# SSD rows in a fourth buffer and asked for earlier, attention steps in another order

## The reference, cut to what matters

```python
a_cs = jnp.cumsum(jnp.moveaxis(a, 2, -1), axis=-1)
seg = a_cs[..., :, None] - a_cs[..., None, :]
Lm = jnp.exp(jnp.where(lower, seg, -jnp.inf)).astype(xs.dtype)
cb = jnp.einsum('bclgn,bcsgn->bcgls', Cc, Bc)
y_diag = jnp.einsum('bcgls,bcgrls,bcsgrp->bclgrp', cb, Lm, x)
```

## Time and profile before

| what | us |
|---|---|
| median of 3 runs (3908.04 to 3921.22) | 3914.33 |
| the profiled execution, whole | 3913.21 |
| its span in the trace | 3911.4 |
| PE busy (12600 matmuls) | 3627.2 (93%) |
| DVE busy | 1151.3 (29%) |
| ACT busy | 767.0 (20%) |
| POOL busy | 428.8 (11%) |
| mean granted TensorE clock, of full speed | 0.978 |

### The profile page before, as it was taken

One profiled execution on the slowest core, in us unless ns is written; L12 is line 12 of the kernel. 1 busy time (PEld: TensorE's weight loads), 2 busy tenths in 40 slices (PEclk: granted clock), 3 DMA queues, 4 the chain that ended last, 5 costly groups with the idle time before them and its releaser, 6 DMA issues.

```text
span 3911.4 us, 33012 instructions
## 1 busy us (share of the span) xinstructions
PE 3627.2 (93%) x12600; PEld 1750.7 (45%) x12600; DVE 1151.3 (29%) x2612; ACT 767.0 (20%) x1772; POOL 428.8 (11%) x393
## 2 busy tenths in 40 slices
PE   8999999999999798788888788999999989999999
PEld 3555555444444433233332344555444545454444
DVE  3355656333201303110111034433221144432211
ACT  2135454223201200000000022222110122221100
POOL 0003324011000000000000002101220021012200
PEclk9899999999999899999999999999999999999999
DMA  8413223112224599999999961012222211122220
GB/s 282 154 61 97 87 72 103 49 56 87 65 65 178 212 409 409 409 409 409 409 409 409 409 236 54 27 44 81 85 76 74 76 54 38 38 92 77 74 81 27
DMA packets 302209, 634.08 MB, mean 162 GB/s; under 512 B 32554, under 2 KB 145818, under 8 KB 301798
## 3 DMA queue, kind: packets, MB, share of 16 engines
q1 hardware_dynamic: 241278, 592.28, 40.7%
q10 hardware_dynamic: 60776, 39.70, 3.7%
HBM read 625.50 MB, written 10.24 MB: 163 GB/s over the span
## 4 chain that ended last, share of the span: by engine, by line
PE 55%; DMA 17%; DVE 3%; SPq 1%; issue 1%; POOL 0%; ACT 0%; DVEq 0%
PE psum L308 27%; DMA arena<-in_w_exp_up_dram 7%; DMA arena<-in_w_exp_gate_dram 6%; PE psum L1638 6%; PE psum L2441 5%; PE psum L2898 4%; PE psum L2934 4%; DMA arena<-in_w_exp_down_dram 4%; PE psum L1462 2%; PE psum L2919 1%; PE psum L1490 1%; PE psum L2367 1%; PE psum L1471 1%; SPq L277 1%; PE psum L2833 1%
## 5 line engine op out<-in xcount | busy, mean ns | idle before, releaser
L308 PE MATMUL psum<-arena 128*128 128x512 f32 (+1 forms) x3200 | 1302.9, 565 | 2.6 <-POOL arena L2040 2.4
L308 PEld LDWEIGHTS psum<-arena 128*128 128x128 f32 x3200 | 609.8, 193 | 675.3 <-issue 653.0
L2441 PE MATMUL psum<-arena 128*64 128x512 f32 x3072 | 692.9, 597 | 141.7 <-DMA arena<-in_w_exp_up_dram 77.1
L2441 PEld LDWEIGHTS psum<-arena 128*64 128x64 f32 x3072 | 232.4, 136 | 583.3 <-issue 567.5
L1638 PE MATMUL psum<-arena 128*128 128x512 f32 x768 | 351.0, 612 | 0.0
L810 PE MATMUL psum<-arena 128*128 128x512 f32 (+1 forms) x768 | 255.9, 491 | 1.1 <-DVE arena L550 1.1
L1638 PEld LDWEIGHTS psum<-arena 128*128 128x128 f32 x768 | 147.0, 195 | 193.4 <-issue 192.5
L1570 DVE CUSTOM_DVE_ANT_0 arena<-psum,arena 128x512 f32<-128x512 f32 (+3 forms) x224 | 113.9, 546 | 391.2 <-PE psum L1462 391.0
L2977 POOL TENSOR_SCALAR arena<-arena 128x512 f32<-128x512 f32 x88 | 138.6, 1576 | 697.7 <-ACT arena L2956 697.7
L810 PEld LDWEIGHTS psum<-arena 128*128 128x128 f32 x768 | 144.4, 191 | 107.9 <-issue 96.1
L2983 DVE SCALAR_TENSOR_TENSOR arena<-arena 128x512 f32<-128x512 f32 x88 | 66.2, 752 | 426.5 <-POOL arena L2977 426.5
(11 more groups left out here) (276 smaller groups left out, 2909.4 us busy)
## 6 DMA issues: line engine op xcount, KB each, us to landing
arena<-in_w_exp_gate_dram SPq DMA_DIRECT2D x128, 1024.0 KB, 18.6
arena<-in_w_exp_up_dram SPq DMA_DIRECT2D x128, 1024.0 KB, 18.5
arena<-in_w_exp_down_dram SPq DMA_DIRECT2D x128, 1024.0 KB, 18.5
arena<-in_w_in_dram SPq DMA_DIRECT2D x64, 1024.0 KB, 5.2
arena<-in_w_up_dram SPq DMA_DIRECT2D x88, 512.0 KB, 4.9
arena<-in_w_ada_dram SPq DMA_DIRECT2D x24, 1024.0 KB, 9.1
arena<-in_w_down_dram SPq DMA_DIRECT2D x20, 1024.0 KB, 5.1
arena<-acs_scratch ACTq DMA_DIRECT2D x64, 256.0 KB, 4.6
```

What stands on the lines that cost most here:

```text
L308: mm = pe.matmul(shaped(b, l, r), l, r, start=kt == 0, stop=kt == nkt - 1)
L2441: mm = pe.matmul(banks[n][64 * j:64 * j + 64, :], lhs[:, kt, 64 * j:64 * j + 64], w, start=kt == 0, stop=kt == 2 * nkb - 1)
```

## The change

The halves with `k % 4 == 3` (n = 3 and 7 of each group) get their rows in two of the `XD` buffers, those which the last two state matmuls of the group have read; `ER` and `RB` serve the other three. The rows of halves n+2 and n+3 are both asked for after the exponents of n and n+1, and none before them. Both transfers of a half are now waited for together, before its first exponent. New waits keep the shared buffers in order: ACT waits for the state matmul 9 of the group before it asks for the rows of n = 3 or 7, DVE and POOL wait for the last use of these buffers before they weigh the sources 2 and 3 of the next group. In the attention DVE takes `weights` of the unit before ahead of `scores`, and POOL does `second` one step earlier, ahead of the filler of the following step.

```diff
--- before.py
+++ after.py
@@ -1121,6 +1121,8 @@
                 wait_xs(e, g)
             if xd_before(u):
                 e.wait_ge(*at(*xd_before(u)))
+            if g and m in (2, 3):
+                e.wait_ge(*(at("yd", g - 1, 3, 1) if m == 3 else at("sel", g - 1, 7)))
             if g == 0 and m < 2:
                 e.wait_ge(*at("ws"))
             first_xd(e, u)
@@ -1165,7 +1167,7 @@
             pe.wait_ge(*at("M", g, n))
             for h in range(4):
                 hh = 4 * hq + h
-                mm = pe.matmul(y[:, hh * 64:hh * 64 + 64], r3(ER[n_of(g, n) % 3], 128)[:, h, :], xs2[g % 2][:, c, hh * 64:hh * 64 + 64], start=True, stop=True)
+                mm = pe.matmul(y[:, hh * 64:hh * 64 + 64], r3(rows_of(n_of(g, n), 0), 128)[:, h, :], xs2[g % 2][:, c, hh * 64:hh * 64 + 64], start=True, stop=True)
             mm.then_inc(*up(S("pe_y"), ("yd", g, c, hq)))
             if hq == 0:
                 return
@@ -1191,15 +1193,18 @@
                 act.wait_ge(*at("acD"))
                 act.wait_ge(*at("gam", 5, 1))
                 act.wait_ge(*at("full", ("row", 5, 1)))
-            if k > 2:
-                act.wait_ge(*at("yd", (k - 3) // 8, (k - 3) % 8 // 2, (k - 3) % 2))
-                act.wait_ge(*at("sel", (k - 3) // 8, (k - 3) % 8))
+            if n % 4 == 3:
+                act.wait_ge(*at("full", ("st", g, 9)))
+            if k > 3:
+                act.wait_ge(*at("yd", (k - 4) // 8, (k - 4) % 8 // 2, (k - 4) % 2))
+                act.wait_ge(*at("sel", (k - 4) // 8, (k - 4) % 8))
             for d in range(2):
                 act.dma_start(r3(rows_of(k, d), 128), acsD[32 * d + h0:32 * d + h0 + 4, c * 128:(c + 1) * 128].partition_broadcast(128)).then_inc(
-                    *up(S(f"rb_in{2 * (k % 3) + d}"), ("rb", g, n, d), by=16))
+                    *up(S(f"rb_in{k % 4}"), *([("rb", g, n)] if d else []), by=16))
 
         def rows_of(k, d):
-            return (RB if d else ER)[k % 3]
+
+            return XD[(2 * (k // 8) + 1 - d) % 4] if k % 4 == 3 else (RB if d else ER)[k % 4]
 
         def act_exponents(act, g, n):
 
@@ -1207,8 +1212,8 @@
             h0, k = 8 * g + 4 * hq, n_of(g, n)
             if k == 0:
                 act.wait_ge(*at("aclog"))
+            act.wait_ge(*at("rb", g, n))
             for d in range(2):
-                act.wait_ge(*at("rb", g, n, d))
                 r_ = rows_of(k, d)
                 for h in range(4):
                     one_head = slice(h * 128, h * 128 + 128)
@@ -1217,7 +1222,7 @@
                         *up(S("act_er"), *([("seg", g, n)] if d and h == 3 else [])))
 
         def act_decays(act, g, n):
-            e = ER[n_of(g, n) % 3]
+            e = rows_of(n_of(g, n), 0)
             act.wait_ge(*at("sel", g, n))
             act.activation(e, e, ACT.Exp, bias=0.0, scale=1.0).then_inc(*up(S("act_exp1"), ("er", g, n)))
 
@@ -1234,10 +1239,8 @@
                     act_two_exponents(act, g, 0)
                 yield
             for n in range(10):
-                if n % 2 == 0 and n < 8:
-                    if n:
-                        load_rows(act, g, n + 1)
-                        act_two_exponents(act, g, n)
+                if n % 2 == 0 and 0 < n < 8:
+                    act_two_exponents(act, g, n)
                 if n == 8:
                     act_square_z(act, g, 1)
                 elif n == 6:
@@ -1254,7 +1257,8 @@
         def act_two_exponents(act, g, n):
             act_exponents(act, g, n)
             act_exponents(act, g, n + 1)
-            load_rows(act, g, n + 2)
+            for m in (2, 3):
+                load_rows(act, g, n + m)
 
         def act_square_z(act, g, c):
             act.wait_ge(*at("u", g, c))
@@ -1345,7 +1349,7 @@
                                          in1=dsk[:, 8 * g:8 * g + 8], op0=ALU.mult, op1=ALU.add).then_inc(*up(S("dve_cb"), ("skip", g, c)))
             k = n_of(g, n)
             dve.wait_ge(*at("seg", g, n))
-            dve.copy_predicated(r3(ER[k % 3], 128), rep(early.bitcast(I32), 4), r3(rows_of(k, 1), 128)).then_inc(*up(S("dve_sel"), ("sel", g, n)))
+            dve.copy_predicated(r3(rows_of(k, 0), 128), rep(early.bitcast(I32), 4), r3(rows_of(k, 1), 128)).then_inc(*up(S("dve_sel"), ("sel", g, n)))
 
         def dve_second(dve, g, n):
 
@@ -1391,7 +1395,7 @@
             mark(("gone", g, "pool"), S("pool_ty"))
 
         def pool_first(pool, g, n):
-            c, e = n // 2, r3(ER[n_of(g, n) % 3], 128)
+            c, e = n // 2, r3(rows_of(n_of(g, n), 0), 128)
             pool.wait_ge(*at("cbt", g, c))
             pool.wait_ge(*at("er", g, n))
             pool.tensor_tensor(e, e, rep(CBB[c % 2], 4), ALU.mult).then_inc(*up(S("pool_M"), ("M", g, n)))
@@ -1618,7 +1622,7 @@
                 dve.scalar_tensor_tensor(out=oT2[:, p, :], in0=PS.of(("o2", J.id, p)), scalar=J.gain, in1=hy, op0=ALU.mult, op1=ALU.mult).then_inc(
                     *up(S("dve_oT"), ("free", ("o2", J.id, p)), ("oT2", J.id, p)))
 
-            yield from att2_steps(J, (1, sums), (0, scores), (1, weights), (2, turned), (3, outs), (4, heads))
+            yield from att2_steps(J, (1, sums), (1, weights), (0, scores), (2, turned), (3, outs), (4, heads))
 
         def pool_att_2(pool, J):
             def second(i, u):
@@ -1626,7 +1630,7 @@
                     pool.wait_ge(*at("lam2", J.id, i))
                     pool.tensor_scalar(J.score(i, 1), J.score(i, 1), sv2(i, 1)[:, 2:3], None, ALU.mult).then_inc(*up(S("pool_S1"), ("S2", J.id, i)))
 
-            yield from att2_steps(J, (0, lambda i, u: J.pool_tables(pool, i)), (1, second))
+            yield from att2_steps(J, (0, lambda i, u: J.pool_tables(pool, i)), (0, second))
```

## The result

The changed kernel takes 3860.3 us (median of 4 runs, 3859.0 to 3861.5), the kernel before 3913.4 (4 runs). The ratio is 0.9863, with a 95% interval from 0.9845 to 0.988: faster by 53 us. 3866 was forecast, within 3845 to 3897.

The account below looks back on a forecast made before the run. PE, busy 93% of the span, was taken as the bound, with only its idle time and clock to win outside the transfer-bound experts. Gains 28.3 + 10.8 + 3.5 + 5.0 = 47.6 us from 3913.2 gave 3866, range 3845 to 3897.

Parts of the forecast that it names:

- SSD, 28.3: SSD: asking for rows earlier removes PE's late wait in all four groups and the slow clock behind it, 28.3 us.
- a term that was set at nothing: SSD: DVE's and POOL's new waits before weighing sources 2 and 3 cost nothing, being already implied by their queues.
- 15.1 of idle time: SSD: PE's waits for half 6 and, in the fourth group, for DVE one pair earlier, 15.1 us over four groups.
- 13.2 of slow clock: SSD: extra time of PE's work at half clock behind those waits, 13.2 us over four groups.
- Rival D: SSD gains nothing, as rows land late or POOL or DVE is next; attention alone, 3894 us; chance 0.10.
- Differential units, 10.8: Second block's differential attention units: the new order gains 6.2 us in the first layer and 4.6 in the second.
- 5.7 in step 9: Differential units: PE waits 5.7 us in step 9, behind scores, rope, eviction, sums, POOL's product and weights.
- The short waits leave the clock up: Differential units: short waits, like earlier ones of 0.76, 1.15 and 1.22 us, would not lower PE's clock.
- Single-softmax units, 3.5 + 5.0: Single-softmax attention units: the copy moves ahead, gaining 3.5 us in the first block and 5.0 in the second.
- B: Attention: DVE's chain takes back all the gain, leaving the SSD's only, 3885 us; chance 0.26.
- C: Attention: the chain never shows and all waits go with their slow clock, 3798 us; chance 0.07.
- E: Differential units of both layers: new waits keep PE at 1.2 GHz throughout, a slower kernel of 3951 us; chance 0.07.

Follow-up runs that it names:

- e9: Kernel before plus four unused 512-column matmuls ahead of PE's wait for the sums' bank, in the first three groups of the SSD: 3915.3 us, ratio 1.0005.
- e2: Kernel before with the new attention order (weights ahead of next scores, POOL's product moved) in the differential units only: 3902.6 us, ratio 0.9984.
- e3: Kernel before with the new attention order (weights ahead of next scores) in the single-softmax units only: 3890.3 us, ratio 0.9954.
- e1: Changed kernel without its attention edits, so the SSD part of the change alone: 3886.6 us, ratio 0.9939 to the kernel before.
- e7: Changed kernel with DVE's projection work (rope, evictions) moved from filled to unfilled differential steps: 3854.8 us, ratio 0.9856 to the kernel before.
- e12: Changed kernel without POOL's product of the second softmax's scores, whose factor is left out: 3841.1 us, ratio 0.9812 to the kernel before.
- e10: Changed kernel with its fourth buffer, but rows asked for where the kernel before asks for them: 3887.0 us, ratio 0.993 to the kernel before.
- e6: Changed kernel with DVE's copy of the turned unit ahead of the next scores, in all attention units: 3826.0 us, ratio 0.9785 to the kernel before.
- e4: Kernel before plus nine unused 512-column matmul calls into the sums' bank ahead of PE's wait for half 6: 3933.5 us, ratio 1.006.
- e8: Changed kernel with DVE's head norms, and the return of their bank, one step later: 3848.0 us, ratio 0.9843 to the kernel before.

## Why the prediction was right, step by step

**SSD, 28.3.** Right in mechanism and nearly in size. The table gives 26.2; what is missing is a term that was set at nothing. PE waits 0.66 us in each of three groups for DVE's weighing (2.0 in all). It is not the new wait of DVE on PE's last sums or on the selection, as far as the trace tells: e9, which lacks these waits, shows the same wait with 2.2 us, so DVE's sums ahead of the weighing make it. The last of them in turn waits for POOL, and takes 1.51 us where 0.69 is usual; which of the two engines is the limit there no run separates:

```profile
347.94 1.51 DVE L1380 TENSOR_TENSOR arena<-arena 128x512 f32<-128x512 f32 x1 [1.60 <-POOL arena L1414]
```

The 15.1 of idle time went whole. The 13.2 of slow clock went whole too, but were not independent of it (the first two groups of e9). The fourth group's 5.1 are not robust: from its first matmul of the states it took 91.3 us here before and 87.7 in e2 and e3, whose SSD is the same. Against those two the gain is 407.8 - 384.1 = 23.7, and e1's runs say 24. Rival D is refuted by e1.

**Differential units, 10.8: measured 9.5** (6.6 and 3.0), but that is luck: errors that cancel. Idle time fell by 8.4 us in the first layer, not by 1.1; slow clock and lost overlap took the difference back. Step by step in the first layer after: waits of 0.18, 0.26, 0.34 in steps 3, 5, 7 (forecast 0.75, 0.95, 1.15), 2.56 in step 9 (5.7), none in 11, 3.24 in 13 (4.0), 0.34 in 15 (1.5).

```profile
2344.62 0.70 PE L1466 MATMUL psum<-arena 32*128 32x256 f32 x4
...
2345.51 0.69 PE L1466 MATMUL psum<-arena 32*128 32x256 f32 x2
2346.39 0.69 PE L1466 MATMUL psum<-arena 32*128 32x256 f32 x2 [0.18 <-DVE arena L1595]
...
2367.93 1.28 PE L1466 MATMUL psum<-arena 32*128 32x512 f32 x2 [0.34 <-DVE arena L1595]
2369.14 5.21 PE L308 MATMUL psum<-arena 128*128 128x256 f32 x16
...
2377.77 0.63 PE L1475 MATMUL psum<-arena 128*128 128x128 f32 x4 [2.56 <-DVE arena L1581]
```

The short waits cost more than they show. A unit's two scores take 0.70 us at 256 columns as a pair (x4), and 0.69 each (x2) when the bank wait parts them: 0.69, 0.91 and 1.12 us are lost besides. With it the bank costs 0.87, 1.17 and 1.46 in steps 3, 5 and 7, above the forecast. A part of that sum, "about 0.25 of signalling", is about 0.1 in the rows: PE goes on at 2367.93, DVE's copy ended at 2367.87.

| first layer, us | forecast | measured |
|---|---|---|
| bank, steps 3, 5, 7 and 15 (waits and parted scores) | 4.4 | 5.0 |
| chain, steps 9, 11 and 13 | 10.0 | 5.8 |
| slow clock | 4.9 | 8.0 |

The last is what is left of the busy time: 74.80, less 72.93 - 10.0 for the same work at full clock, less 3.8 for the parted scores. The sums are 19.2 and 18.8. In the second layer the waits are the same and the slow clock is 10.1.

The step that failed is "5.7 in step 9". The chain's length was right: its links measured 5.01 us for "5.2", and 6.44 with the rope in it, where the terms of the prediction give 6.5. The filler ahead of the wait was slow (5.21 instead of 3.6), which I had excluded behind short waits, and hid 1.5 of it; idle 2.56 and slow 1.5 together are 4.1, and e7, whose filler ran at full clock, waited 0.19 + 3.95. The other 1.6 must lie in where I had put the chain beside PE's steps, which the prediction doesn't write out.

The step "The short waits leave the clock up" is wrong too. The filler behind the wait of 0.34 us in step 7 ran at 0.50 in the changed kernel (5.21 us) and in e12 (5.39), and at 1.00 behind the same wait in e7 (3.73). The filler behind the other wait of 0.34, in step 15, took 8.84 us instead of 7.15 in the changed kernel and in e7. Nor is a wait "of 1.65 us and more" what decides, in the kernel before already: behind the wait of 2.12 us at 2435.00 the filler ran at full clock (3.73 us), and behind the same two waits of 1.15 and 0.40 the values took 2.38 us in the first layer (2555.67) and 3.96 in the second (3368.37). What decides stays open; no size of wait tells it here.

**Single-softmax units, 3.5 + 5.0: measured 8.8 + 11.8.** This is where the prediction was low. Idle time is as forecast (3.9 in the first block, 2.3 a layer, for 3.5 and 2.5). The mis-sized term is the clock, which I had assumed unchanged: its share is 5.0 in the first block and 3.6 a layer, 12 us in all in this pair of profiles, and 5.5 to 20 over all pairs of the two orders. The longer waits fell from 1.8 to 2.8 us to 1.2 to 2.0, and the granted clock went from 0.98 to 1.00, in e3 too, where only this part was changed.

**The sum.** 47.6 forecast, 56.4 measured inside the changed parts: SSD 2.1 less, differential 1.3 less, single-softmax 12.1 more. 4.6 went elsewhere, in code that is the same. So the mechanism of the largest term, the rows, was right and its size nearly so; that the whole comes within 6 us is luck in part, since a clock gain that I had left out stands against losses that I had not foreseen.

**Rivals.** B (the chain takes the attention's gain) is refuted by the attention's 30 us in the stretches, 24 in the runs of e2 and e3. C (no chain) as well: 5.8 us a layer are still waited for weights, and e12, without POOL in the chain, is 17 us shorter in the two layers. E (slower, PE at 1.2 GHz through the differential units) did not come: granted clock 0.90 and 0.88 there, against 0.88 and 0.90 before. (A layer's stretch, which E takes as 85.6 us, is 86.6 in the table; that moves E by 2 us.)

## What to carry to other kernels

Ask when a buffer would be asked for, not only how many there are: the fourth buffer with the old time of asking made the SSD 7 us slower than before, with the new time 26 faster (10 and 24 against the two other profiles with the old SSD). A wait that shrinks can give more than its length, through the clock behind it, but only if nothing else is late right there: look for the next chain before adding the clock's share. Where PE waits for a bank and its owner's copy needs only what PE did a step ago, put that copy ahead of work that needs what PE has yet to do: one exchange in the order, worth 26 to 28 us in the stretches here.

## What the runs showed of the hardware

**Rows land later where weights land beside them.** In the kernel before, the two loads of 256 KB at 326.12 share the engines with two of 1024 KB, and the transfers of this stretch say:

```profile
q1 hardware_dynamic: 1056, 2.10, 56.3%
q10 hardware_dynamic: 1056, 0.52, 17.0%
...
arena<-in_w_in_dram SPq DMA_DIRECT2D x2, 1024.0 KB, 6.7
arena<-acs_scratch ACTq DMA_DIRECT2D x2, 256.0 KB, 8.3
```

In the changed kernel four such loads at 300.5 to 302.5, alone, took 5.7 at the median. In e10 two loads beside the same weights took 9.0. No run moves the weights, so that they are the cause is likely but not shown. The Trainium skill, "DMA: Bandwidth & Descriptors", section "Anatomy of one DMA — SWDGE (gpsimd) path", from which I had 3.2 us, gives its figure for one transfer that GpSimd issues. These loads are ACT's and go by a hardware queue (q10), so the prediction used the figure outside its place, and no run here tests it.

**Two scores on 32 rows run side by side**, 1.13 us for both at 512 columns, 1.12 for each when parted. The Trainium skill, "TensorEngine Tiling (Array Packing)", section "Tiling Modes", says that tiles work in parallel; the trace agrees, and adds that a wait between the two loses it.

**DVE beside POOL.** In e6 DVE's weights took 1.61 us where the same operation takes 0.62 in the changed kernel (at 2364.31), while POOL's product of two tensors ran:

```profile
2350.47 1.26 POOL L1653 TENSOR_TENSOR arena<-arena 128x512 f32<-128x512 f32 x1
2350.55 1.61 DVE L1581 SCALAR_TENSOR_TENSOR arena<-arena 128x384 f32<-128x384 f32 x1 [1.37 <-POOL arena L1631]
```

**The start varies.** From 160 to 200 us, in code that is the same in all kernels, PE's granted clock was 0.70 in the changed kernel's profile, 0.70 to 0.74 in all others, and 1.00 in e4's and e8's, whose starts took 241 us and not 248 to 254. These 10 us are 0.25% of the time, and the reason why distances between PE instructions were read here and not spans alone.
